# Compressed probabilities of two heads in one transpose, with the second key head's compressed values on the other partitions

## The chip, the cores and the metric

The kernel runs on one NeuronCore of a Trainium2 chip, in one launch. The metric is device time in microseconds; before the change three runs gave 942.88, 942.88 and 944.38, median 942.88. All data are 32-bit floats, with bfloat16 for masks only.

## The reference, cut to what matters

One inference step of a hybrid decoder layer, for a prompt of 1024 tokens and for 8 samples of 8 new tokens each. An input projection feeds three groups of heads; their results are gated, projected by `w_out`, added to x and normalised. The prompt's attention is what the change touches. Each of 8 query heads (two key/value heads, four query heads to each) sees three branches: 63 compressed blocks, the selected blocks (for this length all of them, so plain causal attention) and a window of 512 tokens:

```python
def query_block(q0):                       # 128 query rows
    o_c, imp = nsa_cmp_attend(qb, t, kc, vc)        # 63 compressed keys and values
    ...
    o_s = gathered_attend(qb, kg, vg, ...)          # selected blocks
    ...
    o_w = window_attend(qb, t, wb[:, :, 0], wb[:, :, 1], kpos_w)
    return gb[:, :, 0] * o_c + gb[:, :, 1] * o_s + gb[:, :, 2] * o_w
```

Each branch is softmax(q k / 8) v with its own keys and values. Compressed keys and values come from a small network over 32 tokens at a stride of 16. Four further heads attend to 256 memory tokens.

## The kernel before, in words

There are three stages. The trunk (to 482 us) projects x in chunks of columns by three products of high and low parts, and beside it compresses keys and values and computes retention. Attention (482 to 829 us) works on the prompt, with the samples' attention filled in between. The output stage projects and normalises nine tiles.

**Units.** A query tile i has 128 rows, and work for it comes in units (i, l). For l < 16, l // 4 is g, the place of the query head in its key head's group, and l % 2 is j, the key head: units come in pairs of heads (g, j = 0) and (g, j = 1). For l % 4 of 0 or 1 a unit is the selected branch; for 2 or 3 it is the window branch and the compressed branch of a head (two softmaxes, a = 0 and a = 1). l of 16 and 17 are memory heads. `UNITS` lists all 144 (tile 6 with 1, then 7 with 0, 5 with 2, 4 with 3) in `BLOCKS` of four or two.

**One unit, engine by engine.** TensorE writes the scores to PSUM (`qk`, L1687 to L1717), VectorE takes the maxima (`maxima`, L2037), ScalarE the exponentials with their sums into the buffer `P[v % 2]` (L1975); window probabilities lie at column 0 and the 64 compressed ones at column 640, and columns 704 to 768 hold zeros that GpSimd writes once (L2242, semaphore `p_zero`). TensorE transposes the probabilities in tiles of 128 columns, up to four to a chunk, into one of three PSUM banks (`transposes`, L1742). ScalarE or VectorE copies the chunk to one of eight buffers `PTs` (`pt_copy`, L1913). Then `pv` (L1866) multiplies with the values, for both heads of a pair, each into its half of the partitions of bank 7. A product's operand is the value tile with 64 columns; for the compressed branch that is `VC[:, NDB]`, where rows 0 to 63 hold the compressed values (both key heads, 64 columns each) and rows 64 to 127 zeros (L696).

**Order.** `schedule` (L1410) writes one list of steps that every engine walks through and takes its own from. For each unit v: `qk` and `max` of v + 2, the chunks of v (`add_p`), the products of pairs that are complete, the exponentials of v + 2, then one group of the samples' work. Copies of chunks alternate between ScalarE and VectorE by a running turn (L1422, `act_of`). TensorE's scores of v + 2 wait for the exponentials of v; the exponentials of v wait for the transposes of v - 2. A finished block's result is copied (`ot`), and transposed (`o`) after three more chunks (L1433). A sample pair's pages are loaded by SyncE (`load_pair`, L1601) once the product `sv` of the pair before is done. Towards the end of attention ScalarE and VectorE also split the output weights (`w_hi`, L2016, and `w_lo`, L2170).

**Compression.** `second` (L839) makes the compressed values in PSUM, and `keep` (L1061, L1070) copies them to `VC`. `KCp` holds the compressed keys of the prompt; GpSimd copies it to both ends of `KW` (L749, semaphore `p_kw`) and it isn't used after that.

Of the kernel before, what the change touches and what calls it, by code (L numbers as in the profile page):

```python
# [20 lines left out]
F32 = mybir.dt.float32  # L21
# [9 lines left out]
NDB, DS = 8, 8  # L31
# [3 lines left out]
HD = 64  # L35
# [109 lines left out]
def build(nc, io):  # L145
# [4 lines left out]
    def S(name):  # L150
        if name not in sem:
            sem[name] = nc.alloc_semaphore(name)
        return sem[name]
# [17 lines left out]
    fix = Region(nc, BASE, "f_")  # L171
# [4 lines left out]
    ident = fix("ident", [128, 128])  # L176
    identb = fix("identb", [128, 128], BF16)
    colc = fix("colc", [128, 19])
    KCs = fix("KCs", [128, NDB, 64])
    VC = fix("VC", [128, NDB + 1, 128])  # L180
    KCp = fix("KCp", [128, 2, 64], F32R)
    oc_at = fix.at
    OC = fix("OC", [128, NT, 256])
# [20 lines left out]
    psum = nc.alloc_psum_tensor("psum", [128, 8 * 512], F32)  # L204
# [18 lines left out]
    w2 = rc("w2", [128, 2, HD])  # L223
# [35 lines left out]
    NC = 64  # L259
    NPT = 8  # L260
# [6 lines left out]
    QB = [rp("QB0", [128, 12, 128], F32R), nc.alloc_sbuf_tensor_at("p_QB1", [128, 12, 128], F32R, offset=qb1_at)]  # L267
    assert rp.at <= split_at + 2 * (4 * 4 * WMAX) + 2 * (KT * 4 * WMAX) and qb1_at + 12 * 128 * 4 >= split_at + 2 * (4 * 4 * WMAX) + KT * 4 * WMAX
    P = [rp(f"P{i}", [128, T]) for i in range(2)]
    ssum = rp("ssum", [128, 2, 28])  # L270
    gw = rp("gw", [128, 2, 28])
    nb = rp("nb", [128, NNB])
# [4 lines left out]
    PTs = [rp(f"PT{i}", [128, 512]) for i in range(NPT0)]  # L277
# [12 lines left out]
    V = rp("V", [128, 2, QT, 128])  # L290
    KM = rp("KM", [128, 4, NM], F32R)
    VM = rp("VM", [128, 2, 256])
# [401 lines left out]
    def pool_trunk(pool):  # L694
        ch = Link(pool, S("r_pool"))
        pool.memset(VC[64:128], 0.0).then_inc(S("vc_zero"), 1)  # L696
        pool.wait_ge(S("vc_zero"), 1)
        pool.wait_ge(S("x_tr"), 6)
        pool.dma_start(pD[:, :, 0:1], io["page_table"].rearrange("b (p o q) -> (b p) o q", o=1, q=1).to_broadcast([NDB * NPG, NPG, 1]), allow_slow_non_contiguous=True).then_inc(S("row_in"), 16)
        pool.wait_ge(S("row_in"), 16)  # L700
# [7 lines left out]
        for what, n in b_steps:  # L708
# [16 lines left out]
            elif what == "ev":  # L725
                j, t = proj_jobs[n]
# [63 lines left out]
    def pe_trunk(pe):  # L790
# [48 lines left out]
        def second(idx):  # L839
            u, v = item(idx)  # L840
            pe.wait_ge(S("c_gelu"), idx + 1)
            if idx:
                pe.wait_ge(S("c_kv"), kv_count(idx - 1))
            else:
                pe.wait_ge(S("c_const"), 64)
            h = hid[idx % 2]
            nb = 2 if u < NDB // 2 else 1
            for kv in range(2):
                if v == 0:
                    i = nc.tensor.matmul(psum[64 * kv:64 * kv + 64, 512 * 7:512 * 7 + 64 * nb], w2[:, 0], h[:, nb * kv:nb * kv + nb], start=True, stop=True)  # L850
                else:
                    for b in range(nb):
                        o = 512 * 7 + 128 * b + 64 * kv
                        i = nc.tensor.matmul(psum[0:64, o:o + 64], h[:, nb * kv + b], w2[:, 1], start=True, stop=True)
            i.then_inc(S("c_l2"), 1)

        def finish():
# [194 lines left out]
    def dve_trunk(dve):  # L1052
# [8 lines left out]
        def keep(idx):  # L1061
            u, v = item(idx)
            dve.wait_ge(S("c_l2"), idx + 1)
            if u < NDB // 2:
                if v == 0:
                    i = nc.vector.tensor_copy(KCs[:, 2 * u:2 * u + 2, :], bank(7, 128))
                else:
                    i = nc.vector.tensor_copy(VC[0:64, 2 * u:2 * u + 2, :], psum[0:64, 512 * 7:512 * 7 + 256])
            elif v == 1:
                i = nc.vector.tensor_copy(VC[0:64, NDB, :], psum[0:64, 512 * 7:512 * 7 + 128])  # L1070
            else:
                dve.wait_ge(S("c_kcp_hi"), 2)
                nc.vector.tensor_tensor(KCp[64:128, 0, :], psum[0:64, 512 * 7:512 * 7 + 64], KCp[0:64, 0, :].bitcast(F32), ALU.subtract).then_inc(S("c_kv"), 1)
                i = nc.vector.tensor_tensor(KCp[0:64, 1, :], psum[64:128, 512 * 7:512 * 7 + 64], KCp[64:128, 1, :].bitcast(F32), ALU.subtract)
            i.then_inc(S("c_kv"), 1)
# [268 lines left out]
    def softmaxes(v):  # L1344

        i, l = UNITS[v]
        base, at = 1024 * ((v + 1) % 2), sm_before[v]
        if l >= 16:
            m = l - 16
            return [(at + j, 24 + 2 * m + j, 3, 2 * m + j, 0, NM, [(base + 512 * j, NM)], 256 * j) for j in range(2)]  # L1350
        g, j = l // 4, l % 2
        h, k0 = g + 4 * j, 0 if l % 4 < 2 else max(0, i - WIN // 128)
        n = 128 * (i + 1 - k0)
        halves = [(base, n)] if n <= 512 else [(base, n // 2), (base + 512, n // 2)]
        if l % 4 < 2:
            return [(at, 6 * g + j, 0, h, 0, n, halves, 0)]
        if k0 == 0:
            halves = [(base + NC, n)] if n + NC <= 512 else [(base + NC, n // 2), (base + 512 + NC, n // 2)]
            c_at = base
        else:  # L1360
            c_at = base + 512 + (n // 2 if i == QT - 1 else 448)
        return [(at, 6 * g + 2 + j, 1, h, k0, n, halves, 0), (at + 1, 6 * g + 4 + j, 2, h, 0, 64, [(c_at, NC)], 640)]

    def score_parts(v):

# [21 lines left out]

    def tiles_of(v):

        return [(a, k, 128) for a, s in enumerate(softmaxes(v)) for k in range((s[5] + 127) // 128)]  # L1390

    def sample_groups():

# [16 lines left out]
    def schedule():  # L1410
# [53 lines left out]
        for v in range(NV):  # L1464
# [5 lines left out]
            for f in range(0, len(tiles), 4):  # L1470
                mine.append(add_p(v, tiles[f:f + 4]))
                if l >= 16:
                    waiting.append((mine[-1], mine[-1]))
                elif l % 2:
                    waiting.append((partner[len(mine) - 1], mine[-1]))
            partner = mine
            while waiting and (l % 2 == 0 or l >= 16) and waiting[0][1] not in mine:
                pv()
# [198 lines left out]
    def pe_attend(pe, finish):  # L1677
# [3 lines left out]
        last = len(proj_jobs) - 1  # L1681
        assert last % 4 == 0 and all(by_act(j) for j, _ in proj_jobs[last - 3:])

        pe.wait_ge(S("vc_zero"), 1)
        pe.wait_ge(S("p_kw"), 2)

        def qk(v):  # L1687
# [41 lines left out]
        def transposes(c):  # L1729
# [4 lines left out]
            if kind[0] == "p":  # L1734
                _, v, tiles = kind
                sms = softmaxes(v)
                pe.wait_ge(S("p_exp"), sm_count(v) - len(sms) + 1 + tiles[-1][0])
                if v in (2, 3):
                    pe.wait_ge(S("p_zero"), 2)
                for j, (a, k, w) in enumerate(tiles):  # L1740
                    at = sms[a][7] + 128 * k
                    l = nc.tensor.transpose(o[0:w, 128 * j:128 * j + 128], P[v % 2][:, at:at + w], ident[:])  # L1742
            elif kind[0] == "o":
                n = kind[1]
                pe.wait_ge(S("p_ot"), n + 1)
# [94 lines left out]
        first_mem = min(v for v in range(NV) if any(s[2] == 3 for s in softmaxes(v)))  # L1840

        def pv(pair):
            v = p_chunks[pair[0]][1]
            i, l = UNITS[v]
            if pair[0] == p_index[0]:
                pe.wait_ge(S("p_v"), 32)
            if v == first_mem:
                pe.wait_ge(S("p_k2"), 32)
            wait_chunks_read(pe, pair)
            if l >= 16:  # L1850
                sides = [[(p, k, 128) for p, (a, k, _) in enumerate(p_chunks[pair[0]][2]) if a == j] for j in range(2)]
            else:
                sides = [[(p, k, w) for p, (_, k, w) in enumerate(p_chunks[pair[0]][2])]] * 2
            for m in range(len(sides[0])):
                for j in range(2):
                    p, k, w = sides[j][m]
                    vj = v if l >= 16 else v + j
                    a = j if l >= 16 else p_chunks[pair[j]][2][p][0]
                    _, num, b, h, k0, keys = softmaxes(vj)[a][0:6]
                    g = unit_block[vj]  # L1860
                    if j == 0 and k == 0 and num in (0, 6, 12, 18, 24) and g >= 1:
                        pe.wait_ge(S("p_ot"), g)
                    at = 512 * 7 + 128 * ((num - numbers(num // 6).start) // 2)
                    kv = HD * (h // 4)
                    val = VM[:, k, HD * h:HD * h + HD] if b == 3 else VC[0:w, NDB, kv:kv + HD] if b == 2 else V[:, b, k0 + k, kv:kv + HD]
                    i_mm = nc.tensor.matmul(psum[64 * j:64 * j + 64, at:at + 128], val, PTs[p_rank[pair[j]] % NPT][0:w, 128 * p:128 * p + 128],  # L1866
                                            start=k == 0, stop=128 * (k + 1) >= keys, skip_group_check=True)
            i_mm.then_inc(S("p_pv"), 1)

# [82 lines left out]
    def act_attend(act):  # L1952
# [7 lines left out]
        for what, n in p_steps:  # L1960
            if what == "sm":
# [2 lines left out]
                    act.wait_ge(S("p_tr"), last_chunk[v - 2] + 1)  # L1964
                if v == of_tile[i][0] and prev[i] is not None:
                    wait_norm(act, last_block[prev[i]])
                if v < 2 and i > 4:
                    act.wait_ge(S("p_zero"), 2)
                act.wait_ge(S("p_nb"), sm_count(v))
                for s in softmaxes(v):  # L1970
                    g = s[0]
                    dst = P[v % 2][:, s[7]:s[7] + s[5]]
                    if len(s[6]) == 2:
                        dst = dst.rearrange("p (a b) -> p a b", a=2)
                    nc.scalar.activation(dst, s_view(s), ACT.Exp, bias=nb[:, g % NNB:g % NNB + 1],  # L1975
                                         accum_out=ssum[:, par[i], s[1]:s[1] + 1]).then_inc(S("p_exp"), 1)
# [261 lines left out]
    def pool_attend(pool):  # L2238
        ch = Link(pool, S("p_pool"))
        pool.wait_ge(S("h_mm"), len(proj_jobs))  # L2240
        for i in range(2):
            pool.memset(P[i][:, 704:768], 0.0).then_inc(S("p_zero"), 1)  # L2242
        wait_stored(pool, len(proj_jobs) - 1)
        def load_z(i):
            rows = slice(128 * i, 128 * i + 128)
# [126 lines left out]
```

## Time and profile before

| what | value |
|---|---|
| runs | 942.88, 942.88, 944.38 us |
| profiled execution, span from first to last instruction | 942.1 us (no other time of it is given) |
| mean granted TensorE clock | 0.998 |
| instructions | 20736 |
| TensorE matmul busy | 907.5 us, 96% |
| VectorE, ScalarE, GpSimd busy | 520.0, 414.2, 291.1 us |
| transposes of probabilities (L1742) | 656, 98.9 us recorded |

The engine letters are PE (TensorE), PEld (its weight loads), DVE (VectorE), ACT (ScalarE), POOL (GpSimd), SP (SyncE; SPq is its DMA queue). Matmuls are pipelined, so recorded durations of neighbours overlap and their sum is more than the time that they hold the engine. The chain of waits goes back from the last instruction, at each step to what released it or to the instruction before it on its engine, and so counts each moment once. "Idle" with an arrow names what ended an engine's wait.

### The profile page before, as it was taken

How to read it: one execution, taken by the hardware profiler on the slowest of the kernel's cores; microseconds unless marked ns; L12 is line 12 of the kernel's file. 1: busy time of each engine (PE TensorE's matmuls, PEld its weight loads, DVE VectorE, ACT ScalarE, POOL GpSimd, SP SyncE). 2: the span in 40 equal slices, each digit the busy share in tenths (PEclk: the TensorE clock that was granted, in tenths of full speed). 3: DMA queues.
4: the chain of work that ended last, by engine and by line, in shares of the span. 5: the costliest groups of instructions: out<-in, count | busy, mean ns of one | idle time of the engine just before them, and what ended most of it. 6: DMA issues, size and time to landing. Idle time of an engine off the chain costs nothing.

```text
span 942.1 us, 20736 instructions
## 1 busy us (share of the span) xinstructions
PE 907.5 (96%) x7830; PEld 825.0 (88%) x7830; DVE 520.0 (55%) x1302; ACT 414.2 (44%) x1063; POOL 291.1 (31%) x495
## 2 busy tenths in 40 slices
PE   6999999999999999999999999999999999999997
PEld 6999999999999999999988788868887787878885
DVE  5656332323225476545656687676677758844443
ACT  6443221234343101221656666565765657932221
POOL 0223222212214444544253162325222625410000
PEclk9999999999999999999999999999999999999999
DMA  8654422404240544232878068715504142333331
GB/s 231 177 193 135 143 84 109 160 30 121 71 149 23 141 125 141 67 104 71 213 201 202 7 185 259 240 44 150 148 2 140 47 140 75 105 132 137 126 122 67
DMA packets 85076, 118.10 MB, mean 125 GB/s; under 512 B 12914, under 2 KB 67234, under 8 KB 84402
## 3 DMA queue, kind: packets, MB, share of 16 engines
q1 hardware_dynamic: 71522, 73.30, 27.1%
q0 software_dynamic: 10224, 36.20, 11.7%
q10 hardware_dynamic: 3232, 7.28, 2.1%
q8 instruction: 63, 1.03, 0.5%
q14 instruction: 35, 0.29, 0.1%
HBM read 91.68 MB, written 32.02 MB: 131 GB/s over the span
## 4 chain that ended last, share of the span: by engine, by line
PE 79%; DVE 6%; ACT 4%; issue 4%; DMA 2%; POOL 2%; SPq 2%; ACTq 0%; DVEq 0%; POOLq 0%
PE psum L593 8%; PE psum L594 7%; PE psum L595 7%; PE psum L1866 7%; PE psum L1742 6%; PE psum L1715 4%; PE psum L1885 3%; PE psum L1886 3%; PE psum L1887 3%; PE psum L1716 3%; PE psum L834 2%; PE psum L836 2%; PE psum L835 2%; PE psum L817 2%; PE psum L580 2%
## 5 line engine op out<-in xcount | busy, mean ns | idle before, releaser
L593 PE MATMUL psum<-a_whi,f_xhi 128*128 128x256 f32 (+1 forms) x672 | 194.5, 289 | 1.6 <-DVE f_xlo L1059 1.4
L594 PE MATMUL psum<-a_wlo,f_xhi 128*128 128x256 f32 (+1 forms) x672 | 190.3, 283 | 0.0
L595 PE MATMUL psum<-a_whi,f_xlo 128*128 128x256 f32 (+1 forms) x672 | 189.7, 282 | 0.0
L1975 ACT ACTIVATE p_P<-psum,p_nb 128x640 f32<-128x640 f32 (+7 forms) x224 | 124.2, 561 | 41.3 <-DVE p_nb L2043 37.9
L2043 DVE TENSOR_REDUCE p_nb<-psum 128x1 f32<-128x640 f32 (+7 forms) x224 | 110.4, 523 | 50.9 <-PE psum L1716 43.5
L593 PEld LDWEIGHTS psum<-a_whi,f_xhi 128*128 128x128 f32 x672 | 127.1, 189 | 4.1 <-DVE a_wlo L569 1.8
L595 PEld LDWEIGHTS psum<-a_whi,f_xlo 128*128 128x128 f32 x672 | 127.1, 189 | 0.0
L594 PEld LDWEIGHTS psum<-a_wlo,f_xhi 128*128 128x128 f32 x672 | 127.1, 189 | 0.0
L736 POOL DMA_DIRECT2D h_scratch<-a_hst x93 | 51.3, 554 | 213.7 <-DVE a_hst L1120 104.5
L1742 PE MATMUL psum<-f_ident,p_P 128*128 128x128 f32 x656 | 98.9, 275 | 1.6 <-DVE p_PT L1913 0.9
L1742 PEld LDWEIGHTS psum<-f_ident,p_P 128*128 128x128 f32 x656 | 77.1, 141 | 7.6 <-DVE p_PT L1913 2.2
L569 DVE SCALAR_TENSOR_TENSOR a_wlo<-a_wraw,c_gcol,a_whi 128x256 fp32r<-128x256 f32 (+1 forms) x120 | 63.8, 592 | 27.1 <-ACT a_whi L556 26.9
L1129 DVE TENSOR_TENSOR c_ctlo<-psum,c_cthi 128x512 fp32r<-128x512 f32 (+1 forms) x40 | 25.4, 636 | 93.7 <-ACT c_cthi L1014 93.7
L1913 ACT COPY p_PT<-psum 128x512 f32<-128x512 f32 (+3 forms) x107 | 56.3, 526 | 46.0 <-PE psum L1742 45.0
L1866 PE MATMUL psum<-p_PT,p_V 128*64 128x128 f32 x1056 | 71.8, 279 | 1.6 <-issue 1.3
L1014 ACT CAST c_cthi<-psum 128x512 fp32r<-128x512 f32 (+1 forms) x40 | 21.8, 544 | 106.1 <-PE psum L817 106.1
L1866 PEld LDWEIGHTS psum<-p_PT,p_V 128*64 128x64 f32 x1056 | 56.4, 136 | 12.4 <-issue 10.7
L580 PE MATMUL psum<-f_xhi,a_whi 128*128 128x256 f32 x192 | 55.5, 289 | 2.0 <-DVE a_hst L1118 2.0
L2222 POOL TENSOR_TENSOR p_Oi<-p_Oi 128x128 f32<-128x128 f32 x32 | 16.6, 518 | 129.6 <-DVE p_Oi L2065 129.6
L1913 DVE COPY p_PT<-psum 128x512 f32<-128x512 f32 (+3 forms) x109 | 54.5, 500 | 0.6 <-PE psum L1742 0.6
L581 PE MATMUL psum<-f_xhi,a_wlo 128*128 128x256 f32 x192 | 54.0, 281 | 0.0
L582 PE MATMUL psum<-f_xlo,a_whi 128*128 128x256 f32 x192 | 53.8, 280 | 0.0
(335 smaller groups left out, 2137.2 us busy)
## 6 DMA issues: line engine op xcount, KB each, us to landing
a_wraw<-in_w_in SPq DMA_DIRECT2D x24, 512.0 KB, 4.2
h_scratch<-a_hst POOLq DMA_DIRECT2D x72, 128.0 KB, 3.5
s_SG<-in_cache_nsa_slc SPq DMA_DIRECT2D x64, 128.0 KB, 2.1
p_qd<-q_scratch SPq DMA_DIRECT2D x16, 384.0 KB, 7.8
a_xraw<-in_x_prompt SPq DMA_DIRECT2D x8, 512.0 KB, 6.9
s_MK<-in_cache_mem SPq DMA_DIRECT2D x8, 512.0 KB, 9.0
s_WG<-in_cache_nsa_win SPq DMA_DIRECT2D x8, 512.0 KB, 4.5
mix_scratch<-p_zt POOLq DMA_DIRECT2D x8, 512.0 KB, 3.4
```

Source lines behind the costliest of these rows:

```text
L569: ins = nc.vector.scalar_tensor_tensor(out=lo[:, k], in0=raw[:, k], scalar=split_gain(e, 4 * half + k), in1=hi[:, k].bitcast(F32), op0=ALU ...
L580: nc.tensor.matmul(out, wh, hi, start=first, stop=False)
L581: nc.tensor.matmul(out, wl, hi, start=False, stop=False)
L582: return nc.tensor.matmul(out, wh, lo, start=False, stop=last)
L593: nc.tensor.matmul(out, hi, wh, start=first, stop=False)
L594: nc.tensor.matmul(out, hi, wl, start=False, stop=False)
L595: return nc.tensor.matmul(out, lo, wh, start=False, stop=last)
L1742: l = nc.tensor.transpose(o[0:w, 128 * j:128 * j + 128], P[v % 2][:, at:at + w], ident[:])
L1866: i_mm = nc.tensor.matmul(psum[64 * j:64 * j + 64, at:at + 128], val, PTs[p_rank[pair[j]] % NPT][0:w, 128 * p:128 * p + 128], start=k == 0 ...
L1913: copy(PTs[r % NPT][0:w, 0:128 * n], bank(4 + c % 3)[0:w, 0:128 * n]).then_inc(sem, 1)
L1975: nc.scalar.activation(dst, s_view(s), ACT.Exp, bias=nb[:, g % NNB:g % NNB + 1], accum_out=ssum[:, par[i], s[1]:s[1] + 1]).then_inc(S("p_e ...
L2043: nc.vector.tensor_reduce(out=nb[:, g % NNB:g % NNB + 1], in_=s_view(s), op=ALU.max, axis=AX.X if len(s[6]) == 1 else AX.XY, negate=True). ...
```

## The change

The pair's two heads write their 64 compressed probabilities side by side into one buffer `PCM` of 128 columns, head j at column 64 j. Only the second head's unit has a transpose for it. Its result has head 0 on partitions 0 to 63 and head 1 on 64 to 127. The compressed values of key head 1 now lie on partitions 64 to 127 with zeros above, those of key head 0 on 0 to 63 with zeros below, so a product over all 128 partitions picks one head. `PCM` is placed over `KCp`. The zeroing of `P` and its semaphore go. A pair's chunks may now differ in number (5 tiles against 4 for tile 3), and the schedule pairs a surplus chunk with itself.

```diff
+    PCM = nc.alloc_sbuf_tensor_at("p_PCM", [128, 128], F32, offset=kcp_at)
...
     def pool_trunk(pool):
         pool.memset(VC[64:128], 0.0).then_inc(S("vc_zero"), 1)
-        pool.wait_ge(S("vc_zero"), 1)
+        pool.memset(VC[0:64, NDB, HD:128], 0.0).then_inc(S("vc_zero"), 1)
+        pool.wait_ge(S("vc_zero"), 2)
...
     def second(idx):
-                        o = 512 * 7 + 128 * b + 64 * kv
-                        i = nc.tensor.matmul(psum[0:64, o:o + 64], h[:, nb * kv + b], w2[:, 1], start=True, stop=True)
+                        o, r = 512 * 7 + 128 * b + 64 * kv, 64 * kv if u == NDB // 2 else 0
+                        i = nc.tensor.matmul(psum[r:r + 64, o:o + 64], h[:, nb * kv + b], w2[:, 1], start=True, stop=True)
...
     def keep(idx):
-                i = nc.vector.tensor_copy(VC[0:64, NDB, :], psum[0:64, 512 * 7:512 * 7 + 128])
+                dve.wait_ge(S("vc_zero"), 2)
+                nc.vector.tensor_copy(VC[0:64, NDB, 0:HD], psum[0:64, 512 * 7:512 * 7 + HD])
+                i = nc.vector.tensor_copy(VC[64:128, NDB, HD:128], psum[64:128, 512 * 7 + HD:512 * 7 + 128])
...
     def softmaxes(v):
-        return [..., (at + 1, 6 * g + 4 + j, 2, h, 0, 64, [(c_at, NC)], 640)]
+        return [..., (at + 1, 6 * g + 4 + j, 2, h, 0, 64, [(c_at, NC)], 64 * j)]
...
     def tiles_of(v):
-        return [(a, k, 128) for a, s in enumerate(softmaxes(v)) for k in range((s[5] + 127) // 128)]
+        sms = softmaxes(v)
+        if sms[-1][2] == 2:
+            return [(0, k, 128) for k in range(sms[0][5] // 128)] + [(1, 0, 128)] * (UNITS[v][1] % 2)
+        return [(a, k, 128) for a, s in enumerate(sms) for k in range(s[5] // 128)]
...
     def schedule():
-                    waiting.append((partner[len(mine) - 1], mine[-1]))
+                    waiting.append((partner[len(mine) - 1] if len(mine) <= len(partner) else mine[-1], mine[-1]))
...
     def transposes(c):
-                if v in (2, 3):
-                    pe.wait_ge(S("p_zero"), 2)
-                    l = nc.tensor.transpose(o[0:w, 128 * j:128 * j + 128], P[v % 2][:, at:at + w], ident[:])
+                    probs = PCM[:] if sms[a][2] == 2 else P[v % 2][:, at:at + w]
+                    l = nc.tensor.transpose(o[0:w, 128 * j:128 * j + 128], probs, ident[:])
...
     def pv(pair):
-                sides = [[(p, k, w) for p, (_, k, w) in enumerate(p_chunks[pair[0]][2])]] * 2
+                own = [[(c, p, a, k) for p, (a, k, _) in enumerate(p_chunks[c][2]) if a == 0] for c in pair]
+                both = [(pair[1], p, a, k) for p, (a, k, _) in enumerate(p_chunks[pair[1]][2]) if a == 1]
+                sides = [own[j] + both for j in range(2)]
...
     def act_attend(act):
-                if v < 2 and i > 4:
-                    act.wait_ge(S("p_zero"), 2)
+                if v == 2:
+                    act.wait_ge(S("p_kw"), 2)
...
-                    dst = P[v % 2][:, s[7]:s[7] + s[5]]
+                    dst = (PCM if s[2] == 2 else P[v % 2])[:, s[7]:s[7] + s[5]]
...
     def pool_attend(pool):
-        for i in range(2):
-            pool.memset(P[i][:, 704:768], 0.0).then_inc(S("p_zero"), 1)
```

TensorE waits for `vc_zero` at 2 instead of 1 before attention. The remaining lines of `pv` only carry the chunk's index along.

## Rows read from the trace of the kernel before

**Rows 1.** The page's engine summary: busy us, share of span, instructions.

```profile
PE 907.5 (96%) x7830; PEld 825.0 (88%) x7830; DVE 520.0 (55%) x1302; ACT 414.2 (44%) x1063; POOL 291.1 (31%) x495
```

**Rows 2.** Windows: from:to, length, busy us (instructions) by engine, clock, DMA share, GB/s.

```profile
482.30:829.00 346.70, 331.58 (x3407) 280.07 (x3408) 249.53 (x605) 230.49 (x662) 134.78 (x236) 1.00 0.44 131
...
770.00:829.00 59.00, 55.58 (x569) 46.97 (x568) 46.66 (x99) 47.63 (x127) 24.38 (x28) 1.00 0.40 126
```

**Rows 3.** Chain of waits by line: 483 to 829 us, then 829 to 942.

```profile
by line: PE psum L1866 19.3%; PE psum L1742 15.5%; PE psum L1715 9.9%; PE psum L1716 8.0%; issue 7.9%; ACT p_P L1975 4.5%; PE psum L1712 3.3%; PE psum L1726 3.2%; PE psum L1747 2.6%; PE psum L1794 2.6%; PE psum L1819 2.1%; DVE p_nb L2043 2.
...
by line: PE psum L1885 26.5%; PE psum L1886 26.4%; PE psum L1887 26.4%; PE psum L1753 6.3%; PE psum L1882 3.3%; PE psum L1881 3.3%; PE psum L1747 0.8%; ACT d_yo L2029 0.6%; DVE d_yt L2184 0.6%; DVE d_yo L2188 0.6%; PE psum L1866 0.5%; DVE p
```

**Rows 4.** By source line: count, duration ns min/median/max, first and last start, forms.

```profile
L1742 PE MATMUL psum<-f_ident,p_P x656: 270/272/331, 484.4 to 828.0; 128*128 128x128 f32 x164
...
L1866 PE MATMUL psum<-p_PT,f_VC x128: 272/273/273, 494.9 to 826.8; 128*64 128x128 f32 x128
```

**Rows 5.** Pieces of the chain: start us, length us, what.

```profile
488.08 0.66 PE psum L1742 x6
...
617.29 2.08 DMA s_SG<-in_cache_nsa_slc
...
774.53 0.55 PE psum L1742 x5
```

**Rows 6.** Timeline, page loads: start, us, engine, operation, [idle before <- releaser].

```profile
600.07 17.55 SPq L1609 DMA_DIRECT2D s_SG<-in_cache_nsa_slc  x16
...
619.50 0.63 PE L1794 MATMUL psum<-f_ident,s_SG 128*128 128x128 f32 x4 [0.62 <-DMA s_SG<-in_cache_nsa_slc]
```

**Rows 7.** Copies of chunks by shape, attention: busy us, mean ns, idle before.

```profile
L1913 ACT COPY p_PT<-psum 128x512 f32<-128x512 f32 x74 | 43.3, 586 | 34.8 <-PE psum L1742 34.1
...
L1913 ACT COPY p_PT<-psum 128x128 f32<-128x128 f32 x5 | 1.3, 261 | 0.5 <-PE psum L1742 0.5
L1913 DVE COPY p_PT<-psum 128x512 f32<-128x512 f32 x38 | 25.9, 682 | 0.0
L1913 DVE COPY p_PT<-psum 128x256 f32<-128x256 f32 x39 | 16.2, 415 | 0.6 <-PE psum L1742 0.6
...
L1913 DVE COPY p_PT<-psum 128x128 f32<-128x128 f32 x19 | 5.3, 280 | 0.0
```

**Rows 8.** Window of attention, writers of the copied chunks alone: ScalarE, then VectorE.

```profile
482.30:829.00 346.70, 56.28 (x107) 1.00 0.44 131
...
482.30:829.00 346.70, 54.27 (x109) 1.00 0.44 131
```

**Rows 9.** TensorE's waits in attention: line <- releaser: us, times, longest.

```profile
PE psum L1819 <- ACT p_PT L1913: 2.3, 2, 1.2
...
PE psum L1747 <- DVE p_PT L1913: 1.0, 2, 0.7
PE psum L1742 <- DVE p_PT L1913: 0.9, 2, 0.6
```

**Rows 10.** Timeline where attention starts, three engines.

```profile
480.67 1.09 DVE L2043 TENSOR_REDUCE p_nb<-psum 128x1 f32<-128x896 f32 x1 [3.53 <-PE psum L595]
...
481.97 0.26 POOL L2242 MEMSET p_P<- 128x64 f32 x2
...
482.31 1.01 ACT L1975 ACTIVATE p_P<-psum,p_nb 128x896 f32<-128x896 f32 x1 [1.17 <-POOL p_P L2242]
```

**Rows 11.** By source line: the copy of the prompt's compressed values.

```profile
L1070 DVE COPY f_VC<-psum x1: 282/282/282, 290.4 to 290.4; 64x128 f32<-64x128 f32 x1
```

**Rows 12.** Timeline of TensorE, two waits for exponentials.

```profile
800.22 0.23 PE L1712 MATMUL psum<-p_maskb,f_identb 128*128 128x128 bf16 x1 [0.91 <-ACT p_P L1975]
...
808.59 0.36 PE L1715 MATMUL psum<-p_KM,p_QA 128*128 128x256 f32 x1 [0.88 <-ACT p_P L1975]
```

**Rows 13.** Timeline of ScalarE ahead of the second of them.

```profile
805.57 1.04 ACT L2016 CAST d_whi<-d_wraw 128x1024 fp32r<-128x1024 f32 x1
806.50 0.59 ACT L1913 COPY p_PT<-psum 128x512 f32<-128x512 f32 x1
```

More of the change, by code:

```diff
@@ L180, in build @@
     VC = fix("VC", [128, NDB + 1, 128])
+    kcp_at = fix.at
     KCp = fix("KCp", [128, 2, 64], F32R)
@@ L1361, in softmaxes @@
             c_at = base + 512 + (n // 2 if i == QT - 1 else 448)
-        return [(at, 6 * g + 2 + j, 1, h, k0, n, halves, 0), (at + 1, 6 * g + 4 + j, 2, h, 0, 64, [(c_at, NC)], 640)]
+        return [(at, 6 * g + 2 + j, 1, h, k0, n, halves, 0), (at + 1, 6 * g + 4 + j, 2, h, 0, 64, [(c_at, NC)], 64 * j)]
     def score_parts(v):
@@ L1682, in pe_attend @@
         assert last % 4 == 0 and all(by_act(j) for j, _ in proj_jobs[last - 3:])
-        pe.wait_ge(S("vc_zero"), 1)
+        pe.wait_ge(S("vc_zero"), 2)
         pe.wait_ge(S("p_kw"), 2)
@@ L1842, in pv @@
         def pv(pair):
-            v = p_chunks[pair[0]][1]
+            v = p_chunks[pair[1]][1]
             i, l = UNITS[v]
@@ L1850, in pv @@
             if l >= 16:
-                sides = [[(p, k, 128) for p, (a, k, _) in enumerate(p_chunks[pair[0]][2]) if a == j] for j in range(2)]
+                sides = [[(pair[0], p, a, k) for p, (a, k, _) in enumerate(p_chunks[pair[0]][2]) if a == j] for j in range(2)]
             else:
-                sides = [[(p, k, w) for p, (_, k, w) in enumerate(p_chunks[pair[0]][2])]] * 2
+                own = [[(c, p, a, k) for p, (a, k, _) in enumerate(p_chunks[c][2]) if a == 0] for c in pair]
+                both = [(pair[1], p, a, k) for p, (a, k, _) in enumerate(p_chunks[pair[1]][2]) if a == 1]
+                sides = [own[j] + both for j in range(2)]
             for m in range(len(sides[0])):
                 for j in range(2):
-                    p, k, w = sides[j][m]
-                    vj = v if l >= 16 else v + j
-                    a = j if l >= 16 else p_chunks[pair[j]][2][p][0]
+                    c, p, a, k = sides[j][m]
+                    vj = v if l >= 16 else v - 1 + j
                     _, num, b, h, k0, keys = softmaxes(vj)[a][0:6]
@@ L1864, in pv @@
                     kv = HD * (h // 4)
-                    val = VM[:, k, HD * h:HD * h + HD] if b == 3 else VC[0:w, NDB, kv:kv + HD] if b == 2 else V[:, b, k0 + k, kv:kv + HD]
-                    i_mm = nc.tensor.matmul(psum[64 * j:64 * j + 64, at:at + 128], val, PTs[p_rank[pair[j]] % NPT][0:w, 128 * p:128 * p + 128],
+                    val = VM[:, k, HD * h:HD * h + HD] if b == 3 else VC[:, NDB, kv:kv + HD] if b == 2 else V[:, b, k0 + k, kv:kv + HD]
+                    i_mm = nc.tensor.matmul(psum[64 * j:64 * j + 64, at:at + 128], val, PTs[p_rank[c] % NPT][0:128, 128 * p:128 * p + 128],
                                             start=k == 0, stop=128 * (k + 1) >= keys, skip_group_check=True)
```

## The prediction

> **What bounds the kernel now.** I read the engine summary first: TensorE is busy for 96% of the span, VectorE 55%, ScalarE 44% [rows 1]. Busy shares mix stages, so I cut the span where attention begins and ends. From 482.3 to 829 us, the only stretch in which the change removes work from TensorE, it is busy 331.6 of 346.7 us at clock 1.00 [rows 2]. VectorE has 249.5 and ScalarE 230.5. In the last part, 770 to 829, these two are much fuller (46.7 and 47.6 of 59 us) [rows 2]. The chain of waits over attention agrees: its largest shares are the products of probabilities and values (L1866, 19.3%), the transposes of probabilities (L1742, 15.5%) and the scores (L1715 and L1716, 17.9% together); the exponentials hold 4.5% [rows 3]. So TensorE sets the pace, with places in which another engine's result ends last. The rows to watch are the transposes: 656 of them in 164 stretches [rows 4].
>
> A recorded transpose takes 272 ns [rows 4], but neighbours overlap. The chain gives six of them 0.66 us and five 0.55 us [rows 5], so each one holds TensorE for 0.11 us.
>
> **What is removed: 32 transposes.** Every unit of the third kind (l % 4 == 2: window and compressed branch of a pair's first head) has one transpose for its 64 compressed probabilities, padded by 64 zeros. There are 8 query tiles with 4 such units each, so 32. Afterwards they share the transpose of the partner head. 656 transposes become 624: 32 x 0.11 = 3.5 us of TensorE. How much of it is on the path? The chain has 15.5% of 346 us in L1742 [rows 3], 53.6 us, where all 656 would make 72.2 us: 74%. The other quarter stands where TensorE was going to wait anyway. One such place can be named: SyncE issues the page loads of the next sample pair from 600.07 for 17.55 us, the last one lands 2.08 us after 617.29, and TensorE waits 0.62 us for it [rows 5, 6]. SyncE began when the product of the pair before was done, so three of the removed transposes (units 50, 54, 58) only lengthen that wait. I take 3.5 x 0.74 = 2.6 us; the bounds are 0 (all absorbed) and 3.5 (all carried).
>
> The value products stay as many as they are, 128 of their rows with compressed values [rows 4], each over 128 partitions before and after. The second head's product reads another half of the same copied tile. Nothing in number or shape changes: 0.
>
> The Trainium skill, "TensorE: Matmul & The Clock Gate", Part 4 (PE-mode transpose), gives about 275 ns for a transpose in a kernel's context and says that access latency makes up most of it. This trace agrees with that duration (272 ns) and disagrees that a transpose in a row of them costs so much (0.11 us). By the page's figure this part would be an estimate of 32 x 0.275 = 8.8 us.
>
> **Copies out of PSUM.** 28 copies lose one 128-column block, and four go altogether (tile 3, whose third unit had a chunk for the compressed tile alone). Sixteen of the 28 are on VectorE, nearly all from 256 to 128 columns: 415 - 280 = 135 ns each, 2.2 us. Twelve are on ScalarE, (586 - 261) / 3 = 108 ns a block, 1.3 us. The four are VectorE's, 280 ns each, 1.1 us [rows 7]. That is 4.6 us on two engines that mostly aren't the bound. TensorE idled for such copies in 2.3 + 1.0 + 0.9 = 4.2 us [rows 9], of 56.3 + 54.3 = 110.6 us of copying [rows 8], 4%. 4.6 x 0.04 = 0.2 us; between 0 and 1.
>
> **The zeroing that goes.** The first exponential waits for two memsets on GpSimd, since tile 6 needs its zero padding. Its maximum starts at 480.67 and takes 1.09, so it is there at 481.76; the memsets start at 481.97, and ScalarE at 482.31, after 1.17 us of idle that the trace puts down to them [rows 10]. Without them ScalarE can start 0.05 after the maximum, at 481.81: 0.5 us earlier. TensorE's second score group is issued by then and it waits for this exponential, so the 0.5 us is passed on whole; late next is the same exponential, only sooner. Bounds 0.3 and 0.55. The new waits of ScalarE and TensorE, for the copies of compressed keys, are for work done in the projection stage and cost nothing.
>
> **What is added.** VectorE's one copy of compressed values (282 ns [rows 11]) becomes two of 64 columns, each at most a 128-column copy, so at most 0.3 us more. The product that it waited for is 190 us ahead of the first use, and the retention stage that follows it waits on other things. GpSimd zeroes 64 more columns at the very start, at most the 0.26 us of two such memsets [rows 10], ahead of a wait for the sixth group of transposed x; queued behind are the page-table loads for the first gather. If that cover were gone, 0.3 us would be paid. I take 0, bounds 0 and 0.3. The exponentials of compressed scores get one buffer of their own instead of two. Its next writer waits for transposes that stand behind its readers in TensorE's order, so no new wait.
>
> **What is moved.** Copies of chunks go to ScalarE and VectorE by turns. As tile 3 loses four chunks, the turn is flipped from unit 118 to 122 and again from 130 to 134. In these, six 512-column copies go from ScalarE to VectorE, two come the other way, and two one-block copies go to ScalarE. By [rows 7] ScalarE is relieved by 4 x 0.586 - 2 x 0.261 = 1.8 us, and VectorE gets 4 x 0.682 - 2 x 0.280 = 2.2 us more. It is the full stretch, 770 to 829, where ScalarE also converts the output weights (1.04 us each [rows 13]) and delays exponentials: TensorE waits 0.91 us at 800.22 and 0.88 at 808.59 [rows 12]. Ahead of the second wait stand a conversion at 805.57 and a copy of 0.59 at 806.50 [rows 13]; that copy is unit 132's and goes to VectorE, which ends the wait some 0.5 us sooner. Unit 133's copy comes to ScalarE, 0.1 against it. I take 0.4 us, bounds -1.5 (a loss) and +1.5.
>
> **Sum.** 2.6 + 0.2 + 0.5 + 0 + 0.4 = 3.7 us. Behind attention the chain is TensorE's again, 79% in three product lines [rows 3], so an earlier end is passed on. The profiled execution has a span of 942.1 us; the median run is 942.88, so 0.8 us lie around the span. 942.88 - 3.7 = **939.2 us**.
>
> **Rivals.**
> 1. *Absorbed.* The removed transposes only lengthen waits for exponentials, copies and page loads. For it: the page-load place is certain. Against: most of these waits begin with something that TensorE itself released shortly before (a score group, a product) and so move with it. The start's 0.5 and some 0.5 more remain: 941.9.
> 2. *VectorE takes over (slower).* Place: units 119 to 134. The 512-column copies that move there stand ahead of maxima, which release the exponentials. It decides once they delay the loop by more than the other terms give, 3.3 us. If each of the six costs its whole 0.682, 4.1 us, and of the gain only 1 us comes through elsewhere, the time is 942.88 + 3.1 = 946.0; at half that price, 943.9. For: VectorE is busy 46.7 of 59 us there [rows 2]. Against: ScalarE is as full, and was the one waited for [rows 12].
> 3. *ScalarE's relief counts fully.* The waits of 0.91 and 0.88 us [rows 12] close nearly whole, 1.5 instead of 0.4 and with it some of the next ones: 937.7.
> 4. *A transpose costs its recorded time*: 32 x 0.272 = 8.7 instead of 2.6: 933.1. Against: rows 5. It is the result that the page's figure would give, too.
>
> **Chances.** Forecast 0.62, absorbed 0.14, VectorE 0.07, relief 0.15, recorded time 0.02. About 0.2%, 1.9 us, is what can be told from no change. Of the forecast 0.56 lie beyond it, which with relief and recorded time and a little of the absorbed case makes faster 0.75; slower 0.05, most of VectorE's case; the rest, 0.20, within. The range runs from 937.2 (3.5 for transposes, 1.0 for copies, 0.5, and 0.7 for what is moved) to 942.1 (absorbed, a little worse than worked out).
>
> **What would show it.** 624 transposes where L1742 had 656; 212 copies, 105 of them on ScalarE; the first exponential within 0.1 us of its maximum's end; attention shorter by 3 to 4 us and the parts before and after it unchanged; the wait for page loads near 620 us longer by about 0.3. I am wrong if attention shortens by less than 1.5 or over 6 us, if VectorE's maxima have clearly larger shares in the chain between units 118 and 134, or if the start's 0.5 us comes back as a wait for the second exponential.

## The result and the profile after

The changed kernel is slower: median 948.31 us (947.48 to 950.43, six runs) against 943.99 (942.88 to 945.85, six runs) before, a ratio of 1.005 with the 95% interval 1.0038 to 1.0062. The profiled execution has a span of 946.4 us instead of 942.1. 939.2 was forecast; the result is outside the range of 937.2 to 942.1 and on the other side of no change.

The page's engine summary of after, for [rows 1]; then its window of attention and its last part, for [rows 2] (attention now ends 5 us later, so the second line holds less work than the same line of before):

```profile
PE 907.6 (96%) x7798; PEld 824.5 (87%) x7798; DVE 518.0 (55%) x1301; ACT 411.5 (43%) x1061; POOL 288.1 (30%) x494
```

```profile
770.00:829.00 59.00, 52.32 (x500) 44.04 (x497) 42.31 (x88) 42.18 (x114) 21.26 (x28) 0.94 0.33 102
```

TensorE has its 32 instructions less, and yet as much recorded time; the clock in the last part is 0.94 where it was 1.00, which lengthens the records there. By line there are 592 transposes of `P` and 32 of `PCM`, the 624 that were forecast; the recorded duration of one is unchanged:

```profile
L1749 PE MATMUL psum<-f_ident,p_P x592: 270/273/477, 484.8 to 832.4; 128*128 128x128 f32 x198
```

The copies by line, for [rows 7]: 212 of them, 105 on ScalarE, as forecast.

```profile
L1921 DVE COPY p_PT<-psum x107: 268/541/692, 485.9 to 832.9; 128x512 f32<-128x512 f32 x42, 128x128 f32<-128x128 f32 x28, 128x256 f32<-128x256 f32 x25, 128x384 f32<-128x384 f32 x12
L1921 ACT COPY p_PT<-psum x105: 253/585/603, 485.5 to 830.6; 128x512 f32<-128x512 f32 x66, 128x256 f32<-128x256 f32 x15, 128x384 f32<-128x384 f32 x12, 128x128 f32<-128x128 f32 x12
```

TensorE's waits in attention, for [rows 9]. The first line has no counterpart before:

```profile
PE psum L1749 <- DVE p_Oi L2073: 4.0, 1, 4.0
PE psum L1826 <- ACT p_PT L1921: 2.4, 2, 1.2
PE psum L1720 <- ACT p_PCM L1983: 2.3, 5, 0.8
```

**Cutting attention at landmarks.** Single profiled executions of kernels with nearly the same trunk differ by up to 4 us in when attention starts (the first maximum, [rows 10]; 479.96 in e8, 484.12 in e7 below). So I measure from there, to two landmarks: the fourth `sv` (the product of the last sample pair; I take its first row that reads the selected pages `s_SG`) and the first row of the output stage. These rows in before and in after:

```profile
765.07 1.92 PE L1830 MATMUL psum<-s_SG,s_PTS 128*64 128x128 f32 x32
826.98 0.71 PE L1753 MATMUL psum<-f_ident,d_mt 64*128 64x64 f32 x8
```

```profile
481.48 1.09 DVE L2051 TENSOR_REDUCE p_nb<-psum 128x1 f32<-128x896 f32 x1 [4.05 <-PE psum L597]
763.87 1.92 PE L1837 MATMUL psum<-s_SG,s_PTS 128*64 128x128 f32 x32
831.33 0.71 PE L1760 MATMUL psum<-f_ident,d_mt 64*128 64x64 f32 x8
```

| us, one execution each | first maximum at | to fourth `sv` | from there to output stage | attention | attention, against before |
|---|---|---|---|---|---|
| before | 480.67 | 284.40 | 61.91 | 346.31 | |
| after | 481.48 | 282.39 | 67.46 | 349.85 | +3.54 |

Behind attention both have 115.1 us. So the change brings 2.0 us up to the fourth `sv` and then loses 5.55 in one short stretch.

The first of these two numbers can be checked on more executions, because most of the experiments below change something only behind the fourth `sv` (from unit 117 on). Three profiles have before's order of work up to there (before, e2, e7) and eight have after's (after, e1, e3, e4, e8, e9, e10, e11). Time from the first maximum to the same row of the first and of the fourth `sv`, mean and range:

| us | to first `sv` | to fourth `sv` |
|---|---|---|
| before's order, 3 profiles | 114.4 (114.39 to 114.40) | 284.4 (284.40 to 284.49) |
| after's order, 8 profiles | 113.2 (112.97 to 113.51) | 282.6 (282.15 to 282.89) |

The change brings 1.2 us up to the first `sv` and 1.9 up to the fourth. A single profile of after's order is off by up to 0.4 us either way.

**What is in the stretch behind the fourth `sv`.** TensorE's timeline of after, around the wait, and three windows of it (from:to, length, busy by engine, clock, DMA share, GB/s):

```profile
797.71 0.48 PE L1749 MATMUL psum<-f_ident,p_P 128*128 128x128 f32 x1 [4.05 <-DVE p_Oi L2073]
...
800.47 2.34 PE L1874 MATMUL psum<-p_PT,p_V 128*64 128x128 f32 x20
```

```profile
793.60:797.70 4.10, 0.07 (x1) 0.00 (x0) 0.60 (x2) 0.62 (x2) 3.64 (x7) 0.77 0.29 64
797.70:802.60 4.90, 4.89 (x32) 4.50 (x34) 4.39 (x9) 2.20 (x4) 3.47 (x6) 0.50 0.43 125
802.60:812.00 9.40, 8.82 (x90) 7.25 (x87) 7.46 (x15) 7.35 (x19) 1.36 (x3) 1.00 0.41 141
```

A chunk of transposes waits 4.05 us for its PSUM bank, which VectorE frees by normalising block 33 (`p_Oi`). The granted clock falls within this wait, at about 795.8, and stays at its lower level (0.50, 1.2 GHz) until about 802.6. Twenty products take 2.34 us there, and 1.31 in the same shape before. The clock inside the wait, in two shorter windows:

```profile
795.20:795.80 0.60, 0.00 (x0) 0.00 (x0) 0.00 (x0) 0.00 (x0) 0.59 (x2) 0.99 0.00 0
795.80:796.40 0.60, 0.00 (x0) 0.00 (x0) 0.00 (x0) 0.00 (x0) 0.52 (x2) 0.50 0.82 184
```

VectorE in turn waited for GpSimd's mixing of block 31, since there are two `Oi` buffers:

```profile
797.10 0.56 DVE L2073 TENSOR_TENSOR p_Oi<-psum,p_rw 128x384 f32<-128x384 f32 x1 [6.04 <-POOL p_zt L2233]
```

And GpSimd, before and after. Block 31's mixing is the three rows that end in `p_zt`; the 2.81 us instruction opens `fin`, the samples' final mix, which waits for a DMA:

```profile
776.08 0.45 POOL L2222 TENSOR_TENSOR p_Oi<-p_Oi 128x128 f32<-128x128 f32 x1 [9.24 <-DVE p_Oi L2065]
776.61 0.46 POOL L2223 TENSOR_TENSOR p_Oi<-p_Oi 128x128 f32<-128x128 f32 x1
777.15 0.46 POOL L2225 TENSOR_TENSOR p_zt<-p_Oi,p_zt 128x128 f32<-128x128 f32 x1
787.02 2.81 POOL L2314 TENSOR_TENSOR s_on_s<-s_on_s,s_gs 64x1536 f32<-64x1536 f32 x1 [9.41 <-DMA s_om_s<-om_scratch]
```

```profile
785.43 2.81 POOL L2320 TENSOR_TENSOR s_on_s<-s_on_s,s_gs 64x1536 f32<-64x1536 f32 x1 [19.69 <-DMA s_om_s<-om_scratch]
...
794.86 0.56 POOL L2323 DMA_DIRECT2D mix_scratch<-s_zs  x1 [0.29 <-POOL s_zs L2216]
795.44 0.46 POOL L2230 TENSOR_TENSOR p_Oi<-p_Oi 128x128 f32<-128x128 f32 x1
795.98 0.45 POOL L2231 TENSOR_TENSOR p_Oi<-p_Oi 128x128 f32<-128x128 f32 x1
796.51 0.45 POOL L2233 TENSOR_TENSOR p_zt<-p_Oi,p_zt 128x128 f32<-128x128 f32 x1
```

Before, block 31 is mixed while `fin` still waits for its data. After, it stands behind `fin` in GpSimd's order and comes 19 us later. The chain of waits of after runs through this place:

```profile
768.56 7.88 DMA o_scratch<-s_OSp
...
781.73 3.63 DMA s_om_s<-om_scratch
...
785.43 2.81 POOL s_on_s L2320
...
795.44 0.47 POOL p_Oi L2230
...
797.10 0.57 DVE p_Oi L2073
...
797.71 0.69 PE psum L1749 x2
```

**Why the order moved.** `schedule` writes a finished block's `o` and `norm` after three more chunks of probabilities. Unit 118 has one chunk where it had two, so block 31's third chunk is now one of unit 119. Between the two lies unit 118's group of sample work, and that is `fin`.

### The profile page after: what moved, and what is told of

It reads as the page before. It is cut to its first block, busy times and chain, and to the rows that moved or that the text cites. A ratio compares the mean times of both kernels' runs of the same rounds, so it can differ in the third digit from the quotient of the medians.

```text
span 946.4 us, 20664 instructions
## 1 busy us (share of the span) xinstructions
PE 907.6 (96%) x7798; PEld 824.5 (87%) x7798; DVE 518.0 (55%) x1301; ACT 411.5 (43%) x1061; POOL 288.1 (30%) x494
## 4 chain that ended last, share of the span: by engine, by line
PE 72%; DVE 6%; issue 6%; DMA 5%; ACT 4%; POOL 4%; SPq 2%; ACTq 0%; DVEq 0%; POOLq 0%
PE psum L595 7%; PE psum L596 7%; PE psum L597 7%; PE psum L1874 6%; PE psum L1749 4%; PE psum L1895 3%; PE psum L1893 3%; PE psum L1894 3%; PE psum L1723 3%; PE psum L1724 2%; PE psum L837 2%; PE psum L839 2%; PE psum L838 2%; PE psum L582 2%; PE psum L820 2%
## 5 line engine op out<-in xcount | busy, mean ns | idle before, releaser
L1983 ACT ACTIVATE p_P<-psum,p_nb 128x256 f32<-128x256 f32 (+7 forms) x160 | 105.3, 660 | 47.2 <-DVE p_nb L2051 41.7
L1749 PE MATMUL psum<-f_ident,p_P 128*128 128x128 f32 x592 | 93.0, 277 | 5.8 <-DVE p_Oi L2073 4.0
L1749 PEld LDWEIGHTS psum<-f_ident,p_P 128*128 128x128 f32 x592 | 70.8, 141 | 12.1 <-DVE p_Oi L2073 4.3
L1921 ACT COPY p_PT<-psum 128x512 f32<-128x512 f32 (+3 forms) x105 | 53.2, 506 | 43.6 <-PE psum L1749 42.4
L2230 POOL TENSOR_TENSOR p_Oi<-p_Oi 128x128 f32<-128x128 f32 x32 | 14.5, 454 | 126.6 <-DVE p_Oi L2073 126.5
```

Source lines behind the costliest of these rows:

```text
L1749: l = nc.tensor.transpose(o[0:w, 128 * j:128 * j + 128], probs, ident[:])
L1921: copy(PTs[r % NPT][0:w, 0:128 * n], bank(4 + c % 3)[0:w, 0:128 * n]).then_inc(sem, 1)
```

## The experiments

Theory: the loss is block 31's mixing behind `fin`. Rivals: the flipped turn of the copies (VectorE takes over), or something else in the changed schedule or layout. Attention is measured as in the table above; its length in the same kernel run twice differs by 0.4 us (e4, e8). Ratios are against the kernel before on the same chip; they are not quotients of the two medians and differ from those by up to 0.13% (e9).

| kernel | ratio, 95% interval | attention, against before's 346.31 |
|---|---|---|
| after | 1.0050 (1.0038 to 1.0062) | +3.54 |
| e1 after, `fin` later | 0.9984 (0.9973 to 0.9996) | -1.78 |
| e2 before, `fin` earlier | 1.0052 (1.0036 to 1.0069) | +4.74 |
| e3 after, `o` at its old place | 0.9993 (0.9982 to 1.0003) | -2.10 |
| e4 = e1, turn as before | 0.9973 (0.9960 to 0.9986) | -2.36 |
| e5 = e4, 32 transposes more | 0.9998 (0.9983 to 1.0013) | -1.35 |
| e6 = e4, zeroing back | 0.9985 (0.9974 to 0.9995) | -2.58 |
| e7 before, `fin` later | 0.9997 (0.9986 to 1.0008) | -1.56 |
| e8 = e4 again | 0.9980 (0.9970 to 0.9991) | -2.78 |
| e9 = e3, turn as before | 0.9985 (0.9970 to 1.0001) | -2.78 |
| e10 after, filler | 1.0033 (1.0021 to 1.0044) | +3.00 |
| e11 = e4, `fin` later still | 0.9967 (0.9956 to 0.9977) | -2.61 |

**e1, `fin` one group later in the changed kernel.**

```diff
-        groups += [[("load_fin", 0)], [], [("fin", 0)], [], [], [], []]
+        groups += [[("load_fin", 0)], [], [], [("fin", 0)], [], [], []]
```

> The changed kernel with GpSimd's final sample mixing one group of steps later, so that the mixing of block 31 stands ahead of it again. Order theory: the loss is a wait for GpSimd (4.05 us of TensorE idle before 797.71) and the halved clock behind it; both vanish, and the kernel is 3 to 4 us faster than the one before (ratio 0.996 to 0.997). Rival (the new layout itself costs, or the flipped turn of copies does): the time stays above the kernel before, ratio 1.002 or more.

943.37 us, 0.9984: less gain than the 0.996 to 0.997 expected, but well below the rival's 1.002. One empty group of distance takes the whole loss away. GpSimd mixes block 31 at 777.86 again, ahead of `fin`:

```profile
778.92 0.46 POOL L2233 TENSOR_TENSOR p_zt<-p_Oi,p_zt 128x128 f32<-128x128 f32 x1
786.18 2.81 POOL L2320 TENSOR_TENSOR s_on_s<-s_on_s,s_gs 64x1536 f32<-64x1536 f32 x1 [6.80 <-DMA s_om_s<-om_scratch]
```

**e2, the same accident in the kernel before**, `fin` one group earlier and nothing of the change.

```diff
-        groups += [[("load_fin", 0)], [], [("fin", 0)], [], [], [], []]
+        groups += [[("load_fin", 0)], [("fin", 0)], [], [], [], [], []]
```

> The kernel before, unchanged but for GpSimd's final sample mixing one group earlier, so that block 31 is mixed behind it, with none of the change. Order theory: TensorE idles 4 to 7 us near 795 behind VectorE's normalisation of block 33, the clock falls to half for some us, and the kernel is 5 to 8 us slower (ratio 1.005 to 1.009). Rival (the layout costs): no difference, ratio 1.000.

950.08 us, 1.0052: the loss without the change. TensorE's row and the window behind it are those of after:

```profile
798.98 0.69 PE L1742 MATMUL psum<-f_ident,p_P 128*128 128x128 f32 x2 [4.00 <-DVE p_Oi L2065]
```

```profile
799.00:803.60 4.60, 4.60 (x30) 4.21 (x32) 4.08 (x9) 2.20 (x4) 3.43 (x6) 0.50 0.44 122
```

**e3, the other way to the same order**: `fin` stays, and the chunk that tile 3 lost is still counted for waiting `o` steps.

```diff
+            if i == 3 and l < 16 and l % 4 == 2:
+                for o in outs:
+                    o[1] += 1
+                while outs and outs[0][1] >= 3:
+                    write(outs.pop(0)[0])
```

> The changed kernel, with the finished blocks of tile 3 transposed at the place where they stood before (the missing chunk is counted); the sample mixing is not moved, and the turn of the copies stays as changed. Order theory: the same as moving the mixing, ratio 0.996 to 0.997. Rival (layout or turn of copies costs): above 1.002.

944.09 us, 0.9993, attention -2.10; in time again less gain than expected. Two different edits, which share only that block 31 comes ahead of `fin`, both end the wait. With e2 this shows the cause. The turn of the copies stays flipped in e1 and in e3, so it isn't the cause of the loss.

**e4 and e8, the turn of the copies as before**, on top of e1.

```diff
+            if i == 3 and l < 16 and l % 4 == 2:
+                turn[0] += 1
```

> As the first of these (mixing one group later), and the copies of chunks between ScalarE and VectorE in units 118 to 134 by the same turns as in the kernel before. If the flipped turn gave 0.4 us, as predicted, this is 0.4 us slower than the first; if VectorE was overloaded by it, it is faster than the first by 1 us or more.

> The fourth run's kernel again, as the base on the same chip for this group: ratio to the kernel before as it was, 0.996 to 0.999, attention 343.9 us from the first maximum to the first output transpose.

941.84 (0.9973) and, on a second chip, 942.98 us (0.998). The times don't separate these from e1 (0.9984); the profiles do, weakly: attention is 0.6 and 1.0 us shorter, and 0.9 in both in the stretch behind the fourth `sv`, where the turn differs (61.06 against 61.98). TensorE's rows of e1, then of e4:

```profile
791.26 0.33 PE L1749 MATMUL psum<-f_ident,p_P 128*128 128x128 f32 x1 [0.57 <-DVE p_PT L1921]
...
799.39 0.23 PE L1720 MATMUL psum<-p_maskb,f_identb 128*128 128x128 bf16 x1 [0.92 <-ACT p_PCM L1983]
804.35 0.66 PE L1749 MATMUL psum<-f_ident,p_P 128*128 128x128 f32 x4 [0.42 <-DVE p_PT L1921]
807.89 0.36 PE L1723 MATMUL psum<-p_KM,p_QA 128*128 128x256 f32 x1 [0.40 <-ACT p_PCM L1983]
```

```profile
790.64 0.33 PE L1751 MATMUL psum<-f_ident,p_P 128*128 128x128 f32 x1 [0.28 <-DVE p_PT L1923]
...
798.76 0.23 PE L1722 MATMUL psum<-p_maskb,f_identb 128*128 128x128 bf16 x1 [0.91 <-ACT p_PCM L1985]
806.86 0.36 PE L1725 MATMUL psum<-p_KM,p_QA 128*128 128x256 f32 x1 [0.63 <-ACT p_PCM L1985]
```

With the turn flipped (e1) the wait for an exponential near 807 is shorter, 0.40 against 0.63, as the step "what is moved" had it. But two waits for VectorE's copies are longer, 0.57 against 0.28 and 0.42 against none: more is lost than gained. The same flip with `fin` unmoved (e3 has it, e9 below does not) makes no difference in that stretch: 61.40 and 61.38.

**e5, 32 transposes more**, each a second one of a first head's last window tile into the same place, on top of e4.

```diff
+                    again = sms[-1][2] == 2 and UNITS[v][1] % 2 == 0 and c == last_chunk[v] and j == len(tiles) - 1
+                    for _ in range(2 if again else 1):
```

> The fourth run's kernel (mixing one group later, turns as before), with the last window tile of every first head's unit transposed twice: 32 transposes more, in the chunks from which the compressed ones were taken; copies stay short. If a removed transpose brought its 0.08 us on the path, as predicted, attention is 2.6 us longer than in the fourth run; if it brought only the 0.05 us that its profile suggests, 1.5 us; the remainder of the fourth run's gain would then be the copies and the start.

944.07 us, 0.9998 against 0.998 of e8 on the same chip: 1.7 us more by the ratios, whose intervals just overlap, and 1.1 by the medians. Attention is 1.0 and 1.4 us longer than in e4 and e8. The landmarks show where. Against the mean of the eight profiles with after's order, e5 is 0.8 us later at the first `sv` (113.94) for 11 transposes, and 1.8 later at the fourth (284.37) for 25: 0.07 each both times, near the 0.11 x 0.74 = 0.08 of the forecast. That is nearly the whole 1.9 us that the change brings up to there. Behind the fourth `sv`, e5 has 7 transposes more than e4 and e8 and is 0.5 us shorter (60.59 against 61.06); why stays open. Its fourth `sv`:

```profile
765.56 1.92 PE L1841 MATMUL psum<-s_SG,s_PTS 128*64 128x128 f32 x32
```

**e6, the zeroing and ScalarE's wait for it back**, on top of e4.

```diff
+                if v < 2 and i > 4:
+                    act.wait_ge(S("p_zero"), 2)
...
+        for i in range(2):
+            pool.memset(P[i][:, 704:768], 0.0).then_inc(S("p_zero"), 1)
```

> The fourth run's kernel with the two memsets of the probability buffers and ScalarE's wait for them put back. Predicted price of that wait: 0.5 us, all passed on. In the profile the first exponential starts 1.64 us after its maximum starts instead of 1.19, and attention is 0.4 to 0.5 us longer. Rival: it is taken up by the next wait, no difference by the first sample product.

943.58 us, 0.9985; not told apart from e8 (0.998). Attention isn't longer: 343.73, between e4 (343.95) and e8 (343.53). At the first `sv` e6 is 0.2 us later than the mean of the eight profiles (113.40 against 113.2), at the fourth 0.3 (282.87 against 282.6). Both lie inside the range of the eight, so a price between 0 and 0.5 us is neither shown nor excluded.

**e7, `fin` one group later in the kernel before.** The edit is e1's.

> The kernel before with GpSimd's final sample mixing one group later and nothing else. Order theory: block 31 was already mixed ahead of it there, so nothing changes, ratio 0.999 to 1.001, and the gain of the fourth run is the change's own. Rival: the moved mixing is a gain by itself, ratio 0.998 or less, and the change brings correspondingly less.

944.37 us, 0.9997: no difference in time. The one profile has attention 1.56 us shorter, all of it behind the fourth `sv` (60.32 against 61.91), so a part of what e1 gains over before may be `fin`'s place and not the change. Times and profile don't agree here, and it stays open how much.

**e9, both orders as before, `fin` unmoved**: e3's edit and `turn[0] += 1`. It is the change without either of its side effects on the schedule.

> The changed kernel with the whole order of steps as before the change: sample mixing unmoved, finished blocks of tile 3 transposed at their old place, copies by their old turns. Only layout, 32 transposes, copies and the start's wait differ from the kernel before. Prediction without its 0.4 us for the turns: 3.3 us faster, attention 343.0 us. By what the profiles of runs 4 to 8 suggest (0.45 at the start, 1.0 up to the first sample product, little after it) attention is 344 to 345 us against 346.3, and the ratio 0.997 to 0.999.

942.39 us, 0.9985 (0.997 to 1.0001), attention -2.78. This is the nearest measure of what the forecast's first four terms (3.3 us) are worth: 1.4 us by the ratio, 2.6 by the medians (942.39 against 945.00), 2.8 by one profile. With 1.9 in place of this profile's own 2.25 up to the fourth `sv` it is 2.4 (behind it 61.38 against 61.91).

**e10, the wait filled.** In the changed kernel 34 transposes of the identity, whose results nobody reads, stand in front of the chunk that waits.

```diff
+            if kind == ("p", 127, kind[-1]) and c == last_chunk[127]:
+                for _ in range(34):
+                    nc.tensor.transpose(psum[:, 512 * 7 + 384:512 * 8], ident[:], ident[:])
```

> The changed kernel as it is, with 34 transposes of the identity into unused columns of PSUM ahead of the wait that takes 4.05 us; their result isn't used. The wait itself stays. If the halved clock behind the wait is a cost by itself, the granted clock stays at 1.00 from 797 to 803 and attention is 1.5 to 2 us shorter than the 349.85 of the changed kernel. If transposes do not hold the clock, or it costs nothing, attention stays at 349.5 to 350.

948.16 us, 1.0033; the interval overlaps that of after. Attention is 349.31, 0.5 us shorter than in after: neither the 1.5 to 2 nor the nothing that was expected. The filler takes most of the wait's place and the clock stays at its upper level (1.00, 2.4 GHz):

```profile
795.43 3.88 PE L1741 MATMUL psum<-f_ident 128*128 128x128 f32 x34
799.68 0.33 PE L1752 MATMUL psum<-f_ident,p_P 128*128 128x128 f32 x1 [0.38 <-DVE p_Oi L2076]
...
801.18 1.36 PE L1877 MATMUL psum<-p_PT,p_V 128*64 128x128 f32 x20
```

```profile
797.70:802.60 4.90, 4.52 (x51) 3.96 (x49) 3.53 (x7) 0.79 (x3) 4.51 (x9) 1.00 0.33 61
```

From that chunk to the output stage there are 32.46 us (832.14 - 799.68) against 33.62 in after (831.33 - 797.71). So the clock's fall costs some 1.2 us, by one execution of each, and the wait itself 4.05; together 5.2 of the 5.5 us by which e1's last stretch is shorter (61.98 against 67.46). In the whole of attention only 0.5 of the 1.2 shows, since in e10's execution the fourth `sv` came 0.4 us later (282.81 against 282.39), ahead of any difference between the kernels, and the chunk another 0.2 later behind it. The Trainium skill, "TensorE: Matmul & The Clock Gate", Part 4: PE-mode transpose, says that the full clock ("K=8/8") doesn't engage for transposes, which don't count as busy in the same way. This run doesn't bear that out as far as it goes: 34 of them in a row stand where the wait was, and the granted clock, at its upper level before, does not fall. Whether transposes alone would raise it from the lower level, no run here shows.

**e11, `fin` two groups later still**, on top of e4.

> The fourth run's kernel with GpSimd's final sample mixing two groups later still. If what is left of waiting on GpSimd there costs anything (block 32 is mixed behind it), attention is up to 1 us shorter than 343.7; if not, the same time as the fourth run. If GpSimd now delays the output stage's first load, the wait appears before the first output transpose.

941.89 us, 0.9967 (0.9956 to 0.9977), the fastest with e4 (0.9973), from which it is not told apart. Both beat before and after. GpSimd starts `fin` at 785.47, the same moment as in e4 (785.55) to 0.1 us: in both it waits there for its DMA, 7.0 and 6.9 us.

## Why the prediction was wrong

- **What is moved: the step that failed.** It counted turns of copies and went no further. The same lost chunks of tile 3 also set where `o` and `norm` of a finished block are written, and that moved block 31 past `fin` on GpSimd's queue. [Rows 2] show GpSimd busy for 24.38 of the 59 us, which says nothing of an instruction that sits there for 9.4 us waiting for a DMA and holds all behind it. The rule "after three more chunks" was in the text on the kernel before; the list of steps could have been counted through. e1, e2 and e3 show this cause; it costs 5.3 us of attention (after against e1) and 0.66% in time (1.005 against 0.9984).
- **The turns, +0.4 forecast, measured -0.9 with `fin` later and 0 with `fin` unmoved** (the stretch behind the fourth `sv`, e1 against e4 and e8, and e3 against e9). Within the bounds, and no gain in either: [rows 12] showed waits for ScalarE alone. The second of them does end 0.5 us sooner, as worked out (0.40 in e3, 0.90 in e9), but in e1 two waits for VectorE's copies grow by more than its own gain.
- **Transposes, 2.6 forecast, 1.0 to 1.4 in attention's length** (e5 against e4 and e8), 1.1 to 1.7 in time. A transpose does hold TensorE for 0.11 us (e10's 34 take 3.88), not 0.272, so the fourth rival is out. Up to the fourth `sv` the share of 74% was nearly right: 25 transposes were to bring 2.0 us, and 25 more cost 1.8 in e5. The 7 behind it, where ScalarE and VectorE are fullest, were to bring 0.6, and e5 shows nothing of it. Why the stretch is even shorter there is open, and it is one profile. One place was named in the forecast as bringing nothing, the loading of pages, and that is right: in before it ends 24.44 us after the first `sv` (619.50 - 595.06), in after 24.40 (619.04 - 594.64), with three transposes fewer. Yet TensorE's wait for it didn't grow by 0.3, and what took up their time isn't known:

```profile
619.04 0.63 PE L1801 MATMUL psum<-f_ident,s_SG 128*128 128x128 f32 x4 [0.57 <-DMA s_SG<-in_cache_nsa_slc]
```

- **The zeroing, 0.5 forecast.** The place is right: the exponential starts 1.19 us after its maximum (482.67 - 481.48), where it was 1.64 [rows 10], 0.45 sooner. The step "is passed on whole" is not shown: putting the zeroing back (e6) moves the landmarks by 0.2 to 0.3 us, less than equal orders of work differ among themselves.

```profile
482.67 1.01 ACT L1983 ACTIVATE p_P<-psum,p_nb 128x896 f32<-128x896 f32 x1 [0.71 <-DVE p_nb L2051]
```

- **Added work at 0, copies at 0.2**: nothing contradicts them, and no run isolates them.
- **Rivals.** Absorbed, with 1.0 us left of the gain, isn't decided: e9's ratio gives 1.4, its medians and profile 2.6 and 2.8, and up to the fourth `sv` 1.9 us do arrive. VectorE takes over named the right stretch and the engine next to TensorE, and the wrong mechanism: with the turn still flipped, e1 and e3 have no loss. That its 946.0 lies nearest to the measured 948.31 is luck. ScalarE's relief did not count fully: of the two waits of [rows 12] the first stays (0.92 in e1), and only the second shrinks.

The change by itself is worth some 0.15 to 0.3% (e4, e8, e9, e11); with e9's interval reaching to 1.0001, and e7's doubt (all but e9 have `fin` moved as well), not more can be said.

## What to carry to other kernels

When a change alters how many items a scheduling rule counts, write out every engine's list of steps before and after and compare the places, not only the assignments. Then look at each instruction on those queues that waits for a DMA: what changes sides with it inherits its wait. An engine's low busy share hides such an instruction; its longest idle row names it. And to price a small term, compare several profiles at landmarks up to which their order of work is the same: eight of them showed here that one alone is off by up to 0.4 us, nearly the whole price forecast for the zeroing.

## What the runs showed of the hardware

In after TensorE was idle for 4.05 us (4.00 in e2). The granted clock fell to 0.50 while it was idle and stayed there for 4.9 us more (4.6 in e2's window), though TensorE was busy for 4.89 of these 4.90 us; with 34 transposes in the idle place (e10) it stayed at 1.00. The lower clock cost only 1.2 us in the end, since a wait behind it shrank: the next one for an exponential is 0.32 us in after (804.59) and 1.43 in e10.

On GpSimd one instruction's wait held up what stood behind it: in after the engine was idle for 19.69 us in front of `fin`, and block 31's three instructions of 0.46 us each, now behind it, came at 795.44 instead of 776.08.
